# A DeltaNet stage: one broadcast load as four, and the decay stages in earlier slots

## What is computed

```
q, k, v, z, b, a = h @ w_in                    # q, k, v then a causal conv of 4 taps and Silu
beta = sigmoid(b);  g = cumsum(-exp(a_log) * softplus(a + dt_bias))      # within a chunk
decay[i,j] = exp(g_i - g_j) for i >= j, else 0
A = strictly lower part of (beta_i * k_i . k_j) * decay
T = inverse(A + I)
u = T @ (v * beta);  w = T @ (k * beta * exp(g))
for each chunk n:                               # a state of 128 x 128 per head
    v_new = u_n - w_n @ S
    out_n = (q_n * exp(g)) @ S + (q_n k_n^T * decay) @ v_new
    S     = S * exp(g_last) + (k_n * exp(g_last - g))^T @ v_new
o = rmsnorm(out) * silu(z);   result = o @ w_out
```

## Time and profile before

| | us |
|---|---|
| time of the profiled execution | 2209.4 |
| its span | 2207.4 |
| median of three runs (lowest, highest) | 2209.4 (2206.55, 2209.89) |
| DeltaNet stage with its output product, by the chain of PE's work | 1424 to 1829 |
| PE busy in the span | 2144.8 |

### The profile page before, as it was taken

One profiled execution on the slowest core, in us unless ns is written; L12 is line 12 of the kernel. 1 busy time (PEld: TensorE's weight loads), 2 busy tenths in 40 slices (PEclk: granted clock), 3 DMA queues, 4 the chain that ended last, 5 costly groups with the idle time before them and its releaser, 6 DMA issues.

```text
span 2207.4 us, 25975 instructions
## 1 busy us (share of the span) xinstructions
PE 2144.8 (97%) x9662; PEld 1712.9 (78%) x9662; DVE 1058.8 (48%) x1573; ACT 810.2 (37%) x1159; POOL 276.2 (13%) x379
## 2 busy tenths in 40 slices
PE   7999999999999999999999999989999999999997
PEld 6888887756667888888788888768778787888886
DVE  4444444588744444432344442366666454444422
ACT  4333222223554333322333322256565444333221
POOL 1000000123211000000000000045454200000001
PEclk9999999999999999999999999999999999999999
DMA  4333322212112333322233332222231223333321
GB/s 172 95 95 95 112 97 72 73 58 67 48 48 86 100 100 95 113 92 82 85 98 100 97 114 92 72 64 64 50 75 43 67 86 95 95 95 95 114 92 52
DMA packets 55965, 190.17 MB, mean 86 GB/s; under 512 B 11728, under 2 KB 11728, under 8 KB 55888
## 3 DMA queue, kind: packets, MB, share of 16 engines
q1 hardware_dynamic: 53680, 189.00, 27.9%
q10 hardware_dynamic: 2208, 0.13, 0.1%
HBM read 186.74 MB, written 2.36 MB: 86 GB/s over the span
## 4 chain that ended last, share of the span: by engine, by line
PE 88%; DVE 3%; ACT 3%; POOL 2%; DMA 2%; issue 1%; SPq 0%; DVEq 0%; ACTq 0%; POOLq 0%
PE prod L437 27%; PE prod L439 26%; PE prod L438 26%; PE misc L639 2%; DMA blk<-blocks 1%; PE misc L570 1%; PE prod L527 1%; PE misc L588 1%; POOL rows L1510 1%; POOL rows_tmp L1507 1%; DVE w_lo L1055 1%; ACT w_hi L780 1%; PE misc L550 0%; DVE qc L1420 0%; PE misc L579 0%
## 5 line engine op out<-in xcount | busy, mean ns | idle before, releaser
L1055 DVE TENSOR_TENSOR w_lo<-raw,w_hi 128x1024 fp32r<-128x1024 f32 (+1 forms) x300 | 400.9, 1336 | 768.0 <-ACT w_hi L780 767.3
L437 PE MATMUL prod<-h_hi,w_hi 128*128 128x512 f32 x1856 | 760.6, 410 | 0.9 <-DVE w_lo L1055 0.6
L439 PE MATMUL prod<-h_hi,w_lo 128*128 128x512 f32 x1856 | 727.0, 392 | 0.0
L438 PE MATMUL prod<-h_lo,w_hi 128*128 128x512 f32 x1856 | 726.3, 391 | 0.0
L780 ACT ACTIVATE w_hi<-raw 128x1024 fp32r<-128x1024 f32 (+1 forms) x317 | 356.3, 1124 | 606.2 <-PE prod L439 594.5
L437 PEld LDWEIGHTS prod<-h_hi,w_hi 128*128 128x128 f32 x1856 | 350.8, 189 | 101.6 <-issue 35.4
L439 PEld LDWEIGHTS prod<-h_hi,w_lo 128*128 128x128 f32 x1856 | 350.2, 189 | 74.9
L438 PEld LDWEIGHTS prod<-h_lo,w_hi 128*128 128x128 f32 x1856 | 351.3, 189 | 68.4 <-issue 6.0
L437 PE MATMUL prod<-a_hi,w_hi 128*128 128x512 f32 x704 | 278.1, 395 | 0.0
L439 PE MATMUL prod<-a_hi,w_lo 128*128 128x512 f32 x704 | 278.1, 395 | 0.0
L438 PE MATMUL prod<-a_lo,w_hi 128*128 128x512 f32 x704 | 278.1, 395 | 0.0
(11 more groups left out here) (232 smaller groups left out, 1871.2 us busy)
## 6 DMA issues: line engine op xcount, KB each, us to landing
raw<-in_w SPq DMA_DIRECT2D x253, 512.0 KB, 3.5
raw<-in_wd SPq DMA_DIRECT2D x64, 704.0 KB, 4.1
blk<-blocks SPq DMA_DIRECT2D x8, 512.0 KB
x<-in_x SPq DMA_DIRECT2D x8, 256.0 KB, 5.1
out<-y_out SPq DMA_DIRECT2D x8, 256.0 KB, 2.2
consts<-in_consts SPq DMA_DIRECT2D x1, 768.0 KB, 7.7
blocks<-a_mat SPq DMA_DIRECT2D x40, 4.0 KB, 1.4
raw<-in_w SPq DMA_DIRECT2D x2, 256.0 KB, 3.8
```

Of the source, the lines that this page charges most:

```text
L437: pe.matmul(bank, wh, hi, start=first and k == 0, stop=False)
L438: pe.matmul(bank, wh, lo, start=False, stop=False)
L439: ins = pe.matmul(bank, wl, hi, start=False, stop=last and k == tiles_n - 1)
L1055: dve.tensor_tensor(w_lo[:, n % 2, 0:w], raw[:, n % 4, 0:w], w_hi[:, n % 2, 0:w].bitcast(F32), ALU.subtract).then_inc(lo_ready, 1)
```

## The change

Three things are edited. The stages "spread", "decay", "mask" and "tri" of each head from 1 on come 6, 5, 5 and 1 slots earlier (head 0 has them in the same slots as before, by SOONEST). The stages from "turn" to "t7" of head 1 come 2 slots later. And SP issues the load of blk as four, of 32 partitions each, from two blocks each; "rows" waits for all four.

```diff
-CHAIN1 = {"spread": -22, "decay": -19, "mask": -18, "tri": -15, "kk": -13, "amat": -11, "blocks": -10, "lvl5": -9,
+CHAIN1 = {"spread": -28, "decay": -24, "mask": -23, "tri": -16, "kk": -13, "amat": -11, "blocks": -10, "lvl5": -9,
           "qdec": -6, "lvl6": -5, "rows": -4, "rk": -1, "cv": 1, "gram": 5, "lvl7": 5, "turn": 8, "y5": 10, "t5": 12,
           "y6": 14, "t6": 16, "y7": 18, "t7": 20}
...
-LATER = {0: {**{n: 4 for n in TURNED}, **{n: 2 for n in CHAIN2}, "kk": 2, "amat": 2, "blocks": 2, "gram": 1}}
+LATER = {0: {**{n: 4 for n in TURNED}, **{n: 2 for n in CHAIN2}, "kk": 2, "amat": 2, "blocks": 2, "gram": 1},
+         1: {n: 2 for n in TURNED}}
...
                     if g:
                         sp.wait_ge(t_made, g)
-                    sp.dma_start(blk[:].rearrange("p t k j -> p (t k j)"),
-                                 blocks[g].rearrange("b t k j -> b (t k j)").unsqueeze(1)
-                                 .broadcast_to([BLOCKS, BLK, TT * BLK * BLK])).then_inc(blk_in, 16)
+                    for b in range(0, BLOCKS, 2):
+                        sp.dma_start(blk[b * BLK:(b + 2) * BLK].rearrange("p t k j -> p (t k j)"),
+                                     blocks[g, b:b + 2].rearrange("b t k j -> b (t k j)").unsqueeze(1)
+                                     .broadcast_to([2, BLK, TT * BLK * BLK])).then_inc(blk_in, 16)
...
                 elif name == "rows":
-                    pool.wait_ge(blk_in, 16 * (g + 1))
+                    pool.wait_ge(blk_in, 16 * (BLOCKS // 2) * (g + 1))
```

## The result

The changed kernel takes 2249.45 us (median of 4 runs, 2246.14 to 2250.44), the kernel before 2209.64 us in the same series. The ratio is 1.018 with a 95% interval of 1.0163 to 1.0199: **40 us slower**. The forecast was 2271 us (2236 to 2325), slower with 0.84. The sign and the main mechanism hold. Four terms of the sum do not (the rate, the clock and both slot edits), and their errors cancel in part.

The account below looks back on a forecast made before the run. The round of the blocks was taken to set the DeltaNet stage's pace, PE some 2 us behind. Terms: 58 (load) - 6.7 (decay) - 2.5 (head 1) + 13 (clock) = +62 us on 2209.4, so 2271 us, range 2236 to 2325.

Parts of the forecast that it names:

- main mechanism: DeltaNet stage: blk as four loads lands later on two engines, +7.5 us per head, +58 us over the heads.
- Bound of the stage: DeltaNet stage: the round of stores, blk load, rows, t_inv and next a_mat, 35.6 us, sets the pace; PE some 2 us behind.
- Engines: blk load: leading size 2 keeps 2 of 16 DMA engines busy, assumed the same two for all four loads.
- Rate of an engine: blk load: each of two engines moves 262 KB in 13.8 us, so landing takes 15.3 us, where it was 7.8.
- The clock: PE behind the turn: longer idling adds 3.35 us at half speed per head, losing 1.7 us each, +13 us.
- Part 2: Decay moved 5 or 6 slots ahead: state waits (4.9 us) and smaller k wait (1.8 us) behind the turn go, -6.7 us.
- The prices ahead of the turn: Moved decay: new PE waits of 0.8 us for o_rstd and 1.2 us at gram per head, hidden under the t_inv wait.
- Part 3: Head 1, stages from turn on two slots later: PE gets two more slots before its wait, -2.5 us.
- The spread of the four loads: Rival, blk load: the four loads use eight engines, data lands as before, 2200 us; chance 0.12.

## Why the prediction was right, and where its sum was not

- **Bound of the stage.** "The round of the blocks sets the pace": right. The fifth head's round grew by what its load grew (5.5 us), and four loads alone cost 42.5 us. That the rounds grow by the whole of it doesn't hold for all: the five rounds from the third head's a_mat to the eighth's were 37.6 us in the mean and are 41.5, 3.9 us more. The prediction took the fifth head's 35.6 for all of them; they went from 35.6 to 40.3.
- **Engines.** Right: two, and the same two for all four loads.
- **Rate of an engine.** Mis-sized. I took 19.0 GB/s from the first microsecond of blk alone on eight engines; two engines run at 25.5, and four at 23.5. The prediction itself named this as a sign of being wrong ("if the two engines run at 25 GB/s (then near 2244)"), and the time is indeed near that. Its other sizes were too high with it: POOL's wait is 70.2 us and not 85, PE's at the turn 37.1 and not 60. The landing is 13.4 us, not 15.3: +5.5 us per head, not +7.5. By the rate alone it would be 11.8, so with the right rate the sum would have been 1.5 us a head short; the mean rate, landing included, is 22.1 GB/s. With 5.5 the term is 8 x 5.5 - 2 = +42 us, not +58. That the four loads alone measured the same +42.5 is in part luck: there the loads grew by 48.9 us, and shorter pieces behind them gave some of it back.
- **The clock, +13 us.** Mis-sized, and it came with a gain that I had booked elsewhere. The stage from 1424 to 1790 us of the changed kernel and of the one with four loads only:

```profile
1424.00:1790.00 366.00, 302.26 (x1699) 256.35 (x1698) 187.04 (x398) 179.75 (x341) 143.68 (x297) 0.93 0.18 55
```

```profile
1424.00:1790.00 366.00, 295.25 (x1658) 252.28 (x1657) 185.14 (x392) 193.00 (x346) 145.32 (x297) 0.89 0.18 55
```

  Before, the same stretch has 0.95. A mean of 0.93 is 0.14 x 366 = 51 us at the lower level (1.2 GHz), 0.95 is 37 and 0.89 is 81. So the changed kernel spends 14 us more there (7 us of PE work at most), where I took 27 (13). The clock does fall behind a late turn, as forecast (0.50 from 1642 to 1644, the turn at 1641.70). With four loads only, the kernel spends 44 us more at the lower level, 22 us of work at most, and yet the time rose by less than the loads grew. Part of the slow stretch is idling itself; another part is offset, since from t_inv to the next a_mat that kernel takes 11.5 us in the mean of six rounds, and the kernel before 12.2: the lost speed is there, but the state waits aren't. How the 22 us divide was not measured, so what the clock cost stays open. The slots have a part in it too: with the slots alone the same stretch has 0.97.
- **Part 2, -6.7 us behind the turn.** This step failed. The state wait does go in the changed kernel, but it goes with the load alone too; and with the slots alone it stays. The work that was to go from ACT did go (in the changed kernel no table load stands before e_row, at 1626.86), but no wait behind the turn went with it: in the kernel with the early decay alone the state wait is 6.4 us, the k wait of 1.8 us stays, and the one of 4.2 goes, the reverse of the forecast. Alone it costs 2.1 us. The prices ahead of the turn were near: 0.8 + 1.2 us per head forecast, (4.8 + 1.1 + 12.2) / 8 = 2.3 measured, and under the late load they cost nothing that can be told (2249.45 against 2251.65). Without it they were to cost 0.1 to 0.6 us a head; both slot edits alone cost 4.4 us.
- **Part 3, -2.5 us.** This step failed too: the turn's wait shrank by 2.6, and the waits for u_inv and v_new rose to 4.6, from 1.3 at those two places. I had looked at a_mat(2) alone and not at new0 of head 1.
- **Sum.** Four loads alone +42.5 as measured, slots -2.2 beside it (2249.45 against 2251.65, whose intervals overlap, so this isn't told from nothing). The forecast's +62 was 22 us high: 16 from the rate and the rest from the clock and from Parts 2 and 3 together.
- **Rivals.** The spread of the four loads is out. The rule that decided this case, one number in an access pattern, was named from a row (a share of half for a size of 8) and extended to 2. That all four loads would take the same two engines was an assumption when it was made; the sign hung on it, and only the runs showed it.

The best version run is the kernel before with eight loads of one block: 2204.83 us, 0.2% (0.13 to 0.31%) faster than before and 44.6 us faster than the changed kernel. With two queues it takes the same time.

## What to carry to other kernels

A DMA that is cut in pieces must be looked at by its outermost size, not by its bytes: here 8 x 16 x 4 KB ran on eight engines, 2 x 16 x 4 KB on two, and 16 x 4 KB on more than eight. The DMA share of a moment in which the transfer is alone, times 16, gives the number of engines, as long as they aren't waiting for the next issue. A rate per engine wants a stretch of several microseconds, and a sum over all rounds beside the one round that was looked at. Before a stage is moved in several in-order queues, each of its results must be followed to all who wait for it, also those a head later; and a wait that vanishes beside a longer one must not be booked to the edit that was meant to remove it.

## What the runs showed of the hardware that I had not expected

Eight engines that read eight blocks 16 times each are slower one by one than two or four that do the same: 19.0 and 15.8 GB/s each in the two microseconds in which that load is alone, against 23.5 with four and 25.5 with two. In total that is 164 and 139 GB/s with eight, 94 with four and 49 with two: from two engines to four it nearly doubles, from four to eight it grows by half to three quarters. The 11.6 GB/s that the prediction read from the microsecond from 1567 isn't a steady rate: the two microseconds from 1567.3 have 123 / (16 x 0.46) = 16.7. Whether the source or the destination limits it was not tried.

A weight load that is issued right behind blk on the same queue landed 1.1 us behind it with one load, with two and with four: at 1607.3 against 1606.24 before (8.3 us after its issue), at 1618.7 against 1617.66 with two loads (9.1 us), at 1629.2 against 1628.08 in the changed kernel (11.9 us). One without a blk load just ahead of it (issued at 1607.0, before) landed after 3.6 us. So a load on few engines also holds up the wide one behind it; the four buffers hid that here.
